# Attention in two bursts a pair of heads, its sums half a pair later, and four other reorderings

## What is computed

```python
def reference(x, ...):
    x = first_block(x, ...)      # mLSTM heads, pooling, two gated branches, w_out, norm, residual
    return second_block(x, ...)  # below

# second_block, 16 meta tokens ahead of the 256 (L = 272)
hn = rmsnorm(concat(meta, x)); a_q, a_k, a_v, a_g, b_cq, b_ckv, b_kr, b_g = split(hn @ w_in)
# A: 8 heads, softmax of two halves of the features
w = p[:, :, 0] - lam * p[:, :, 1];  oA = rmsnorm(w @ vA) * (1 - lam_init) * silu(a_g)
# B: 8 heads, latent attention with rotary part
oB = softmax((q_nope k_nope + q_pe k_pe) * scale) @ vB * silu(b_g)
h = h + concat(oA, oB) @ w_out;  y = rmsnorm(h)[meta tokens dropped]
```

## Time and profile before

| | us |
|---|---|
| median of 3 runs (lowest, highest) | 1442.43 (1441.68, 1443.58) |
| the profiled execution | 1441.72 |
| its span, first to last instruction | 1440.0 |
| PE busy | 1423.8 (99%) |
| DVE busy | 880.4 (61%) |
| ACT busy | 703.2 (49%) |
| POOL busy | 67.8 (5%) |
| HBM, mean | 184 GB/s |
| 474 copies `wh` (L960), each | 1.059 |
| 474 subtractions `wl` (L1274), each | 1.231 |

### The profile page before, as it was taken

The page is one execution under the profiler, slowest core; times in us unless marked ns, Lnnn a source line. Parts: engine busy times, 40 slices in busy tenths (PEclk is TensorE's granted clock), DMA queues, the critical chain, the costliest instruction groups (busy, mean ns, idle before and its releaser), DMA issues.

```text
span 1440.0 us, 27081 instructions
## 1 busy us (share of the span) xinstructions
PE 1423.8 (99%) x10492; PEld 1344.5 (93%) x10492; DVE 880.4 (61%) x1070; ACT 703.2 (49%) x925; POOL 67.8 (5%) x99
## 2 busy tenths in 40 slices
PE   8999999999999999999999999999999999999997
PEld 8999988899999999999999999888999998888886
DVE  5778774546766777546455556557555546667754
ACT  6555545455555533444344444446433345777643
POOL 1000000001010100000000000001000002111000
PEclk9999999999999999999999999999999999999999
DMA  8565555655556556555666666656655553334553
GB/s 288 176 205 181 194 179 180 204 183 179 163 173 203 179 176 190 173 194 185 206 194 190 193 195 235 237 165 220 205 176 162 178 183 124 117 124 152 207 196 125
DMA packets 72657, 265.96 MB, mean 185 GB/s; under 512 B 8168, under 2 KB 8432, under 8 KB 71664
## 3 DMA queue, kind: packets, MB, share of 16 engines
q1 hardware_dynamic: 70848, 253.65, 54.3%
q0 software_dynamic: 1440, 10.63, 2.1%
q10 hardware_dynamic: 288, 0.52, 0.1%
HBM read 260.56 MB, written 4.20 MB: 184 GB/s over the span
## 4 chain that ended last, share of the span: by engine, by line
PE 96%; DVE 2%; ACT 1%; issue 1%; DMA 0%; DVEq 0%; ACTq 0%; POOL 0%; SPq 0%; POOLq 0%
PE ps L373 21%; PE ps L377 21%; PE ps L375 21%; PE ps L365 8%; PE ps L366 8%; PE ps L367 8%; PE ps L492 2%; PE ps L795 1%; PE ps L584 1%; PE ps L595 1%; DVE wl L1274 1%; ACT wh L960 1%; PE ps L633 0%; PE ps L801 0%; PE ps L799 0%
## 5 line engine op out<-in xcount | busy, mean ns | idle before, releaser
L1274 DVE TENSOR_TENSOR wl<-raw,wh 128x1024 fp32r<-128x1024 f32 x474 | 580.8, 1231 | 482.1 <-ACT wh L960 470.2
L960 ACT ACTIVATE wh<-raw 128x1024 fp32r<-128x1024 f32 x474 | 498.4, 1059 | 522.2 <-PE ps L377 387.7
L373 PE MATMUL ps<-xh,wh 128*128 128x256 f32 x1568 | 436.6, 278 | 0.4 <-DVE wl L1274 0.4
L375 PE MATMUL ps<-xl,wh 128*128 128x256 f32 x1568 | 434.8, 277 | 0.0
L377 PE MATMUL ps<-xh,wl 128*128 128x256 f32 x1568 | 434.6, 277 | 0.0
L373 PEld LDWEIGHTS ps<-xh,wh 128*128 128x128 f32 x1568 | 295.5, 188 | 0.9 <-issue 0.8
L375 PEld LDWEIGHTS ps<-xl,wh 128*128 128x128 f32 x1568 | 295.6, 189 | 0.1
L377 PEld LDWEIGHTS ps<-xh,wl 128*128 128x128 f32 x1568 | 295.5, 188 | 0.0
L373 PE MATMUL ps<-x2h,wh 128*128 128x272 f32 (+1 forms) x432 | 124.1, 287 | 1.0 <-DVE avt L1457 0.4
L377 PE MATMUL ps<-x2h,wl 128*128 128x272 f32 (+1 forms) x432 | 123.3, 285 | 0.0
L375 PE MATMUL ps<-x2l,wh 128*128 128x272 f32 (+1 forms) x432 | 122.9, 284 | 0.0
(11 more groups left out here) (369 smaller groups left out, 2285.0 us busy)
## 6 DMA issues: line engine op xcount, KB each, us to landing
raw<-in_w_stream SPq DMA_DIRECT2D x474, 512.0 KB, 4.0
xn<-in_x SPq DMA_DIRECT2D x8, 256.0 KB, 6.2
xr<-in_x POOLq DMA_DIRECT2D x1, 2048.0 KB, 12.6
x_kept<-xr POOLq DMA_DIRECT2D x1, 2048.0 KB, 9.0
x1r<-x_kept POOLq DMA_DIRECT2D x1, 2048.0 KB, 10.3
out<-yn SPq DMA_DIRECT2D x6, 256.0 KB, 3.4
mrow<-bound_rows POOLq DMA_DIRECT2D x8, 128.0 KB, 3.7
poolw<-in_pool_w POOLq DMA_DIRECT2D x1, 1024.0 KB, 5.2
```

Source lines behind the costliest of these rows:

```text
L373: pe.matmul(out_at(j), whr[:, c, f], hi(kc)[:, tokens], start=st, stop=False, skip_group_check=True)
L375: pe.matmul(out_at(j), whr[:, c, f], lo(kc)[:, tokens], start=False, stop=False, skip_group_check=True)
L960: act.activation(slot_view(wh_at[r], layout), raw[r][:, :, :], ACT.Copy).then_inc(wh_done, 1)
L1274: tt(slot_view(wl_at[r], layout), raw[r][:, :, :], slot_view(wh_at[r], layout).bitcast(F32), ALU.subtract).then_inc(split_done, 1)
```

## The change

- The start: 18 warming turns instead of 12, one piece of x turned ahead of the stream and 16 warming turns behind it; pieces 1, 2 and 3 are turned ahead of slots 1, 2 and 3. ACT and DVE split slot 0 before the parts of x. The second half of piece 0 is asked for on ACT's queue.
- WO to CKQ: the first three of each row's four sums are added ahead; the row's mean is one instruction. The last two rows of x1 come behind the first low parts.
- cq's and g's slots are written at column 0 with pitch 512.
- AK, AV: the first slot of a group goes by columns too, and banks 0 and 1 are emptied in the last slot.
- G: PE has, ahead of slot 0, scores of the pair, sums of A of the pair before, and its B weights turned; ahead of slot 2, sums of B of the pair before and the mixed weights turned. Both sums share bank 7. Squares move to slot 0 (late), A's norm to slot 1, B's to slot 3. The wait for both kept halves of uv moves from slot 2 to slot 0 of the first pair.
- G to W2: `GATED_AT`, `TURNED_AT`, the banks and waits of the turns, the scaling of the last gate group (now ahead of the split of w2 slot 0) and the last gate's product (w2 slot 2) move. Work of the last pair now runs through w2 slots 0 to 3.

```diff
-             "v": TOKEN_RAMP, "wo": BY_TOKEN, "uv": BY_TOKEN, "w2": BY_TOKEN, "ckv": SECOND_KEYS,
+             "v": TOKEN_RAMP, "wo": BY_TOKEN, "cq": BY_TOKEN, "g": BY_TOKEN, "uv": BY_TOKEN, "w2": BY_TOKEN, "ckv": SECOND_KEYS,
              "ak": SECOND_KEYS, "av": SECOND_KEYS, "aq": SECOND}
-EQUAL_PLACES = ((16, 528), (48, 528))

...
-        of = [EQUAL_PLACES[k % 2] if kind in ("cq", "g") else LAYOUT_OF.get(kind, BY_FEATURE)
-              for kind in kinds for k in range(slots_of(kind))] * times
+        of = [LAYOUT_OF.get(kind, BY_FEATURE) for kind in kinds for _ in range(slots_of(kind))] * times
...
-GATED_AT = (("g", 0), ("g", 5), ("w2", 1), ("w2", 1))
-TURNED_AT = (("g", 6), ("w2", 0), ("w2", 2), ("w2", 4))
-TURNED_BANK = (2, 4, 0, 4)
+GATED_AT = (("g", 0), ("g", 6), ("w2", 1), ("w2", 3))
+TURNED_AT = (("g", 5), ("g", 7), ("w2", 3), ("w2", 5))
+TURNED_BANK = (2, 2, 0, 4)
...
-            by_columns = half and k == kcs // SLOT_KC - 1
+            by_columns = half and k in (0, kcs // SLOT_KC - 1)
...
-                    if by_columns and (c, j) == (SLOT_KC - 1, 1):
+                    if by_columns and k > 0 and (c, j) == (SLOT_KC - 1, 1):
...
-            for m in range(TOK):
+            for m in range(TOK if n else 1):
...
-        warm(12)
+        warm(18)
         x_turn(0)
-        x_turn(1)
+        warm(16)
...
-            if j == 0 and k in (1, 2):
+            if j == 0 and k in (1, 2, 3):
                 pe.wait_ge(s_x_low, 2)
-                x_turn(k + 1)
+                x_turn(k)
...
+            o = ps[:, 7, half * S:half * S + S]
...
             if t == 1:
-                pe.wait_ge(pair["kept_m"], H)
+                pe.wait_ge(s_out_low, 1)
             if t == 2:
                 pe.wait_ge(s_gsum, 4)
             if t == 3:
-                pe.wait_ge(s_out_low, 2)
+                pe.wait_ge(pair["kept_m"], H)
             for c in range(4):
...
             if k == 0:
-                if first >= 1:
-
-                    pe.wait_ge(pair["kept_m"], p)
-                    weighted(6, vbn, p - 1, pair["sums_m"])
                 if here:
                     if first < 1:
                         pe.wait_ge(s_qp, 1)
+                        pe.wait_ge(s_uv_kept, 2)
                     else:

                         pe.wait_ge(pair["max_m"], p)
                     scores(p, odd)
-            if k == 2 and here:
-                pe.wait_ge(pair["mix"], p + 1)
                 if first >= 1:
-                    pe.wait_ge(pair["normed_m"], p)
-                else:
-                    pe.wait_ge(s_uv_kept, 2)
-                turned(wmix, pair["turned_d"])
-            if k == 3 and here:
-                pe.wait_ge(pair["kept_d"], p + 1)
+
+                    pe.wait_ge(pair["kept_d"], p)
+                    if first >= 2:
+                        pe.wait_ge(pair["normed_m"], p - 1)
+                    weighted(0, avn, p - 1, pair["sums_d"])
+                    pe.wait_ge(pair["exp_m"], p)
+                    turned(pm[1 - odd], pair["turned_m"])
+            if k == 2:
                 if first >= 1:
+
+                    pe.wait_ge(pair["kept_m"], p)
                     pe.wait_ge(pair["normed_d"], p)
-                weighted(7, avn, p, pair["sums_d"])
-                pe.wait_ge(pair["exp_m"], p + 1)
-                turned(pm[odd], pair["turned_m"])
+                    weighted(1, vbn, p - 1, pair["sums_m"])
+                if here:
+                    pe.wait_ge(pair["mix"], p + 1)
+                    turned(wmix, pair["turned_d"])

         def attention(q, k):
-            if isinstance(q, int) and q == 3 and ("g", k) == TURNED_AT[0]:
-                turn_gated(0)
             quarter(q * 2 + k // 4, k % 4, k // 4)
+            if isinstance(q, int) and q == 3 and ("g", k) in TURNED_AT:
+                turn_gated(TURNED_AT.index(("g", k)))

...
-                    if k < 2:
-                        quarter(H, k, 0)
+                    quarter(H, k, 0)
                     if ("w2", k) in TURNED_AT:
                         turn_gated(TURNED_AT.index(("w2", k)))
-                    pe.wait_ge(s_out_low, k // 2 + 1)
+                    pe.wait_ge(s_out_low, max(k // 2 + 1, 2))
...
+        act.dma_start(xn[:, 1, 0:COLS], x[P:2 * P, 0:COLS]).then_inc(s_x[0], 16)
...
+        split(0, 0, LAYOUTS[0])
         x_high_parts(0)
-        split(0, 0, LAYOUTS[0])
         split(1, 1, LAYOUTS[1])
-        x_high_parts(1)
         split(2, 2, LAYOUTS[2])
...
+            if k == 0 and late:
+                if first >= 1:
+                    act.wait_ge(pair["sums_d"], p)
                     for m in range(TOK):
+                        act.activation(ond[:, m, :], ps[:, 7, m * P:(m + 1) * P], ACT.Square,
+                                       scale=stat[:, b1 + 12 + 2 * m:b1 + 13 + 2 * m],
+                                       accum_out=stat[:, b1 + 18 + m:b1 + 19 + m])
+                    act.drain().then_inc(pair["squares"], 1)
+                if here:
                     act.wait_ge(pair["max_d"], p + 1)
                     exps([(sbd[:, c, lo:lo + w], stat[:, b + 4 + 2 * t + c:b + 5 + 2 * t + c],
                            stat[:, b + 8 + 2 * t + c:b + 9 + 2 * t + c], 0.125)
                           for t, (lo, w) in enumerate(((0, K0), (K0, L2))) for c in range(2)], p, pair["exp_d"])
+                if first >= 1:
+                    keep(pair["kept_m"], pair["turned_m"], p)
+            if k == 1 and first >= 1 and not late:
+                act.wait_ge(pair["scale"], p)
+                for m in range(TOK):
+                    act.activation(oall[:, bass.ds(p - 1, 1), m * P:(m + 1) * P].rearrange("p o s -> p (o s)"),
+                                   ps[:, 7, m * P:(m + 1) * P], ACT.Copy, scale=stat[:, b1 + 24 + m:b1 + 25 + m])
+                act.drain().then_inc(pair["normed_d"], 1)
+            if k == 2 and here and not late:
+                if first >= 1:
+                    act.wait_ge(pair["sums_m"], p)
+                keep(pair["kept_d"], pair["turned_d"], p + 1)
             if k == 2 and here and late:
                 act.wait_ge(pair["max_m"], p + 1)
                 exps([(pm[odd][:, lo:lo + w], stat[:, b + 28 + t:b + 29 + t], stat[:, b + 30 + t:b + 31 + t],
                        MLA_SCALE) for t, (lo, w) in enumerate(((0, K0), (K0, L2)))], p, pair["exp_m"])
+            if k == 3 and first >= 1 and not late:
+                act.wait_ge(pair["sums_m"], p)
+                act.wait_ge(pair["inverse_m"], p)
                 for m in range(TOK):
+                    act.activation(oall[:, bass.ds(p + H - 1, 1), m * P:(m + 1) * P].rearrange("p o s -> p (o s)"),
+                                   ps[:, 7, S + m * P:S + (m + 1) * P], ACT.Copy,
+                                   scale=stat[:, b1 + 32 + m:b1 + 33 + m])
+                act.drain().then_inc(pair["normed_m"], 1)

...
+                if k in (1, 2, 3):
+                    x_high_parts(k)
+                for n in ((0,), (), (1,), (2,), (3,), (), (), ())[k]:
                     x_squares(n % 2, n // 2)
...
+        def keys_half(kind, j, b):
+            to = ak if kind == "ak" else avt
+            tt(to[:, 4 * j + 2 * b:4 * j + 2 * b + 2, :], ps[:, 2 * b:2 * b + 2, 0:L2], r1_over(2),
+               ALU.mult).then_inc(psum_free[b], 1)
+
+        def gates_scaled(i):
+            dve.wait_ge(slots_done, FIRST["G"] + (i + 1) * GROUP)
+            for m in range(TOK):
+                last = ts(gates[:, bass.ds(i * 4, 4), m * P:(m + 1) * P],
+                          ps[:, m, :].rearrange("p (c d) -> p c d", d=P), stat[:, 28 + m:29 + m], None, ALU.mult)
+            last.then_inc(s_gsum, 1)
+
...
+            if k == 0 and late and first >= 1:
+                dve.wait_ge(pair["squares"], p)
+                ts(stat[:, b1 + 20:b1 + 22], stat[:, b1 + 18:b1 + 20], 1.0 / P, EPS, ALU.mult, ALU.add).then_inc(
+                    pair["mean"], 1)
+            if k == 1 and not late:
...
+            if kind in ("ak", "av") and k == GROUP - 1:
+                dve.wait_ge(s_keys_half, (2 if kind == "av" else 0) + j + 1)
+                keys_half(kind, j, 0)
...
-                if (kind, k) == GATED_AT[2]:
-                    out_gated(2)
+                if (kind, k) == ("w2", 0):
+                    gates_scaled(3)
...
-                row_mean(m, s_out_mean)
+                ts(stat[:, 20 + m:21 + m], stat[:, 15 + 4 * m:16 + 4 * m], 1.0 / D, stat[:, 34 + m:35 + m], ALU.mult,
+                   ALU.add).then_inc(s_out_mean, 1)
...
+            dve.wait_ge(s_out_squares, 3)
+            for m in range(TOK):
+                dve.tensor_reduce(stat[:, 34 + m:35 + m], stat[:, 12 + 4 * m:15 + 4 * m], AX.X, ALU.add)
+            drain()
+            ts(stat[:, 34:36], stat[:, 34:36], 1.0 / D, EPS, ALU.mult, ALU.add)
+            drain()
...
-            x1_rows(1, range(3))
+            x1_rows(1, range(2))
             x2_low_parts(0)
-            x1_rows(1, [3])
```

(54 more changed lines are left out.)

48 lines of the change are left out of this document (12 added, 36 removed).

## The result

The changed kernel takes 1449.28 us, median of 5 (1443.58 to 1450.3), against 1443.58 for the kernel before in the same comparison (1441.68 to 1445.4): ratio 1.0036, 95% interval 1.0025 to 1.0047. It is slower, by 5.7 us. The forecast was 1441.4, with 0.13 for slower. Four of its five runs lie between 1449.11 and 1450.3; the fifth took 1443.58, as much as the kernel before, and no trace shows what it did otherwise. The profiled execution took 1449.69, 7.97 more than the 1441.72 of before. Its span is 1447.9.

The account below looks back on a forecast made before the run. The prediction took PE, busy 99% of the span, to bound the kernel. Its eight terms summed to -1.0 us, giving 1441.4 us from the runs' median of 1442.43, with an 8-in-10 range from 1438.3 to 1444.9.

Parts of the forecast that it names:

- step 1: Start: earlier first matmul and full clock, against a later turn and a stall; -1.2 us, bounds -1.8 and +0.6.
- 2. The mean: Behind the last WO matmul: three of four sums added earlier shorten the chain PE waits for; -0.2 us.
- 3. Places: CQ and G: weights at place 0 change the matmul pace by about nothing; -0.2 us, bounds -1.7 and +1.4.
- 4. Keys: Ends of key and value groups: banks 0 and 1 emptied earlier remove stalls; -2.0 us, bounds -2.3 and -1.5.
- 5. Bursts: Attention in G: same fp32 work, 22 bursts instead of 27, so five fewer restarts; -0.5 us.
- 6. The mix: G: waits for mixed weights gone, -0.5, but normed_d late by 0.2 in two pairs; net -0.1 us.
- 7. The wait at the first gate slot: First scores: PE newly waits for both kept halves of uv; +1.8 us, bounds +1.6 and +2.0.
- 8. The last gates: G to W2: old wait gone, -1.3, new stall at g 7, +2.5, later turns +0.2; net +1.4 us.
- 1: Rival: the added waits do not bite, as what they ask for is there sooner; 1437.1 us, chance 0.1.
- 2: Rival: fixed places run at V's later pace, and block 3 lands sooner; 1439.3 us, chance 0.12.
- 3: Rival: the clock falls at the start as before, or turns never raised it; 1442.7 us, chance 0.13.
- 4: Rival: the clock falls in the two new stalls; 1445.6 us, or 1443.5 with one fall; chance 0.12.

Follow-up runs that it names:

- e1: The kernel before with the change's start alone; 1446.98 us, ratio 1.003 (6 runs).
- e2: The changed kernel with the old start, all else of the change kept; 1445.67 us, ratio 1.0022 (10 runs).
- e3: The changed kernel with the split of the mLSTM gates' weights made one QK group later; median 1447.84 us, ratio 1.0036 (8 runs).
- e4: The kernel before with one extra 128x128 turn ahead of the last slot of the second QK group; 1447.96 us, ratio 1.0034 (5 runs).
- e11: The kernel before with e4's turn and QK's weights written at column 16 instead of 0; 1452.11 us, ratio 1.006 (4 runs).
- e12: The kernel before with only the halves of the keys and the output's mean; 1440.08 us, ratio 0.9979 (11 runs).
- e5: The kernel before with one extra turn ahead of the last slot of each of seven QK groups; 1448.33 us, ratio 1.0034 (5 runs).
- e10: The kernel before with new start (QK 1 from ramped x, gate weights' split later), output's mean and keys' halves; 1439.97 us, ratio 0.9977.
- e7: The changed kernel with uv's wait back ahead of slot 2 and the gated heads' second quarter at g 5; 1444.53 us (one execution).
- e9: The changed kernel with the changes of e3, e6, e7 and e8 together; 1438.89 us, ratio 0.9971 (7 runs).
- e8: The changed kernel with cq's and g's weights at their old places; 1448.81 us (one execution).
- e6: The changed kernel with the second pair of QK groups fed from the ramped x again; 1445.78 us, ratio 1.0016 (10 runs).

## Why the prediction was wrong, step by step

**The step that failed.** It is step 1 of the prediction, the start. I costed it at its own place, up to slot 4, and put the rest of QK at nothing, since nothing in it changes. But the new order left ACT and DVE 1.5 us later against PE in the second group, where DVE takes 2.89 a slot to PE's 2.72. Some 0.1 us of wait came out, which alone would be nothing; behind it 50 slots took 0.107 more each, 5.4 us. Shown by e1 and e2 (the start makes it), e3 (without the late split it isn't there, in the profiled execution) and e4 (a break alone makes it). Why PE has two paces stays open.

The 233.1 and 226.9 ns in V are a matter of places, as I took them: in every trace V's first three slots have 233, whichever pace QK had, and in e11, which has their weights at 16 too, they have 227. The trace of before has no sign of a second pace: the QK slots that run at 118 and more in it are those with x on the ramp.

**1. The start, -1.2.** First matmul at 11.08, not 10.7, and slot 4 at 25.93, not near 25.0. The clock came up by turns and held, as said, but later than said. Windows of PE in the kernel after, which answer to the earlier trace rows (turns in the first two, the first slot in the third):

```profile
3.30:7.10 3.80, 3.80 (x18) 1.00 0.92 275
8.50:10.30 1.80, 1.80 (x17) 1.00 0.95 358
11.08:14.05 2.97, 2.97 (x25) 1.00 1.04 411
```

The 1.00 of the first row says nothing, for the trace's first entry of the clock is at 7.98 us. Its turns are 0.21 us apart, those of the second row 0.11. The turns up to 7.97 all go at the slower step, and the clock is up from 7.98 to behind the last matmul. In the eight profiled kernels with the new start it is up from 6.3 to 9.5 us on, with nothing but turns ahead. In the six with the old start the first slot begins at 1.2 GHz every time, and the clock is up for good only from 15.7 to 18.9. The Trainium skill ("TensorE: Matmul & The Clock Gate", Part 4) says that the full clock does not engage for turns in transpose mode; these traces do not agree. The waits for x's low parts were 1.3 in all against my 0.8. And the five slots behind the turn ahead of slot 3 have the slower pace in all eight profiled kernels with the new start: from slot 3 (at 22.4 to 23.0) to the second group they take 14.5 us, against 13.8 in before, e2 and e12. That is 0.6 which I had not counted. It is 14.4 in e4 and e5, so behind the turn ahead of slot 2, the last with the old start, it goes either way. The profiled pair shows -0.04 for the start as a whole. But the second group begins at 37.52, 38.72, 38.51, 38.28 and 39.60 in five executions with the old start and the usual places, mean 38.5, and at 36.90 to 37.49, mean 37.2, in eight with the new one. By these the start is worth 1.3; I had set it against the best of the old ones, because the sum was made on one profile. But 1.3 is likely too much: the profiled execution is the slowest of its runs in e4, e5, e11 and e12, and the medians of e10 and e12 leave 0.6.

**2. The mean, -0.2**: -0.18. Right. CQ, where I had nothing, took +0.7: the diagonal for r1 is 0.4 late, behind a raw block for which ACT waited 2.4 (1.8 before). With the new mean and the new order of x1's rows seven profiled executions have it, at +0.6 to +1.0 (e12, which has no new start, among them), and two, e7 and e9, do not; with the old order it is -0.1 to +0.3. So it goes with the new order more often than not, through the landing of that block. No run was made on it, and its cause is open.

```profile
994.99 1.06 ACT L957 ACTIVATE wh<-raw 128x1024 fp32r<-128x1024 f32 x1 [2.43 <-DMA raw<-in_w_stream]
```

**3. Places, -0.2**: +0.2 from UQ to the end by e8, and by the means of cq some +0.1 in CQ. Slots with x2 at 16 and 32 run at 232 to 233 and those at 48 and 0 at 228 to 230, where equal places have 229 to 232. So the mean comes out a little above that of before and not below it. My bounds were also drawn unevenly: 480 matmuls at 3.1 ns are 1.5 us to either side.

**4. Keys, -2.0**: -1.99. Right; no gap at the ends of ak and av. The stretch that answers to the earlier trace rows:

```profile
1125.64 0.29 PE L374 MATMUL ps<-x2h,wl 128*128 128x272 f32 x1
1125.77 0.28 PE L370 MATMUL ps<-x2h,wh 128*128 128x256 f32 x1
1125.88 0.28 PE L372 MATMUL ps<-x2l,wh 128*128 128x256 f32 x1
```

Two steps take 0.24, as anywhere.

**5. Bursts, -0.5**: wrong. The pairs in the middle of G take 0.00 to 0.09 more than before, not 0.06 less. The restarts are 0.2 shorter in a pair, of which 0.1 is a longer restart behind the first of the old bursts (0.2); but the bursts themselves are 0.2 longer: 4.39 and 1.58 beyond a plain step, against 3.73, 0.47 and 1.58 before. I had taken work to be the same wherever it stands.

**6. The mix, -0.1**: the old waits are gone and twice 0.25 stands for the norm behind a sigmoid, 0.0. Right within 0.1.

**7. The wait at the first gate slot, +1.8**: 2.08, just over the upper bound of 2.0. The mechanism is right, shown by e7. The row that answers to the earlier trace rows:

```profile
1207.82 0.94 PE L792 MATMUL ps<-ak,qst 128*128 128x144 f32 x4 [1.83 <-ACTq L1080]
```

**8. The last gates, +1.4**, with 2.5 at g 7: the stall is 2.1 as a wait of PE and 2.3 by the starts against e7. The chain was as I traced it, and e7 takes it away by filling DVE's wait at g 5. Two slots behind PE's later turns begin 0.2 late each, 0.4 in all, against my 0.2. Without the two stalls my terms 5, 6 and 8 leave -1.7; from UQ to the end e7 shows -0.5 and e9 -0.6. The bursts are 0.5 of what is missing; the rest I can't divide.

**The rivals.** 1 and 2 did not come. 3 is refuted by the windows above. 4 came in e3 and e6, 1.6 us for one fall behind the 2.1 stall, and not in the profiled execution of after: in five traces with the same stall it goes either way, and I had given it as one outcome or the other. None of the five had the pace of PE in an unchanged stretch, so the range, up to 1444.9, missed the time by 4.4. A second miss is smaller: all terms but the start's summed to +0.2, and e2 shows 2.4 for them. Of the 2.2 between, 0.7 is CQ, 0.2 the wait at the first gate slot, and 1.2 the bursts, the mix, the places and the last gates.

## What to carry over

In a kernel that PE bounds at 99%, count matmuls in a window of every long stretch, not only waits: a pace 4% slower shows neither as a wait nor in the clock, and over 50 slots it outweighs everything that was reordered. Before moving work ahead of a steady loop, look for the slot where the helper engine is already slower than PE, and leave it its slack; and put a stretch that is known to bring the fast pace back behind each point where PE may be broken. Make the sum for a start against the mean of several executions, not against the one that was profiled.

## What the runs showed of the hardware

- The same 256-column fp32r matmuls, with the same operands and places, run at one of two paces, 113.3 or 117.7 ns between starts, both at full clock with PE always busy. Why is open.
- In the traces with QK's usual places the pace changes only at a break, of 0.05 us at the least, and at the slots whose x stands on the ramp (places 0 to 12, mod 64). A break moved PE from the faster to the slower pace at the first turn of e4 and of e5, at a late split in after, e1, e6, e7 and e8, and at the turn ahead of slot 3 in e3, e7 and e8; the six later turns of e5 left it there. One late split of e6 moved it back. Behind the turn ahead of slot 2 it is 113.3 in six traces and 117.7 in seven, so no rule for a single break comes out. Two slots on the ramp brought back the faster each time: at the second group of QK in the ten traces whose first group ended slow, and at the third in e6. In e9 and e10 the third group was fast already.
- The Trainium skill ("TensorE: Matmul & The Clock Gate", "Back-to-back issue gap") gives a formula for an isolated gap at full clock, by which an estimate for 256 columns is 256/2.4 + 2.5 = 109.2 ns; by rows here it is 113.3 at best, and it has no second pace.
- Places of both operands set the pace, but not by a rule that these runs give: weights at 0 and x at 16 have 113.3 or 117.7, both at 16 have 120; 512-column matmuls with the tokens stationary have their best, 226.9, with both at 16. Why is open.
- Behind a stall of 2.1 us at g 7 the clock fell to 1.2 GHz for 3.4 us in two of five profiled executions, and cost 1.6 us each time.
- Nothing but turns brought the clock up in the eight profiled kernels with 18 and 16 warming turns, 3.1 to 5.2 us behind the first of them.
